# Remainders of weights on one engine, and scores of two attention jobs at once

## What is computed

```python
def first_block(x, ...):
    for i in range(2):
        h = rms_norm(x, norm_g[i])
        z = h @ w_in[i]
        z_a, z_b, z_c = split_cols(z, (RWKV_IN_WIDTH, DSA_IN_WIDTH, DIL_IN_WIDTH))
        y = jnp.concatenate([rwkv7_branch(z_a, ...), dsa_branch(z_b, ...), dilated_branch(z_c, ...)], axis=-1)
        x = x + y @ w_out[i]
        gate = jax.nn.sigmoid(rms_norm(x, ple_norm_g[i]) @ ple_w_gate[i])
        x = x + gate * (p[i] @ ple_w_proj[i])
    return rms_norm(x, final_norm_g)

def second_block(x, mem, ...):
    for l in range(2):
        h = rms_norm_2(x, attn_norm[l])
        # layer 0: o_mix = sparse attention (compressed, selected, windowed; 12 heads)
        # layer 1: o_mix = forgetting_attention(q, k_sh, v_sh, dcum)     (12 heads)
        o_mem = memory_attention(q_mem, mem, mem_norm[l], w_mem_kv[l])   # 4 heads
        x = x + jnp.concatenate([o_mix, o_mem], axis=-1) @ w_o[l]
        x = x + conv_ffn(rms_norm_2(x, ffn_norm[l]), w_up[l], conv_w[l], conv_b[l], w_down[l])
    return rms_norm_2(x, final_norm)

def conv_ffn(h, w_up, conv_w, conv_b, w_down):
    u = h @ w_up                                  # 1024 -> 2 x 2816
    u = causal depthwise convolution of width 3 over u, + conv_b
    a, b = u[..., :D_FF], u[..., D_FF:]
    return (jax.nn.silu(a) * b) @ w_down
```

## Time and profile before

| | |
|---|---|
| median of 3 runs | 1552.84 us (1551.9 to 1553.16) |
| the profiled execution, its own time | 1553.33 us |
| its span, first to last instruction | 1551.4 us |
| mean granted clock of TensorE | 0.853 of 2.4 GHz |
| HBM read, mean rate | 164.9 MB, 107 GB/s |

### The profile page before, as it was taken

How to read it: one execution, slowest core, us unless ns; L and a number is a source line. 1 busy time by engine, 2 the same in 40 slices (tenths; PEclk the granted TensorE clock), 3 DMA queues, 4 the chain that set the end, 5 groups by cost and what they waited for, 6 DMA issues and landing times.

```text
span 1551.4 us, 25100 instructions
## 1 busy us (share of the span) xinstructions
PE 1340.0 (86%) x10545; PEld 1223.1 (79%) x10545; DVE 897.6 (58%) x1579; ACT 648.6 (42%) x1144; POOL 495.3 (32%) x294
## 2 busy tenths in 40 slices
PE   3969885989698859879899899986988999999787
PEld 3957774988577749779777699885988878999787
DVE  1884647457746474557755446777436344588842
ACT  3533123465331235554532345454434333555541
POOL 1544100334440003346400224444545201344541
PEclk9989966999799659889855599998989856999989
DMA  6324100344330004326210144443534301444450
GB/s 242 133 102 141 56 2 1 114 159 136 109 131 29 2 1 169 130 82 234 73 55 1 44 147 136 136 154 131 182 132 139 132 1 55 139 161 163 153 179 35
DMA packets 24448, 167.56 MB, mean 108 GB/s; under 512 B 2704, under 2 KB 2832, under 8 KB 8336
## 3 DMA queue, kind: packets, MB, share of 16 engines
q1 hardware_dynamic: 24336, 165.96, 30.8%
HBM read 164.90 MB, written 1.05 MB: 107 GB/s over the span
## 4 chain that ended last, share of the span: by engine, by line
PE 37%; DVE 16%; ACT 7%; issue 2%; POOL 0%; DMA 0%; DVEq 0%; ACTq 0%; SPq 0%
PE ps L445 7%; PE ps L440 7%; PE ps L442 7%; DVE ARENA L2038 5%; PE ps L603 4%; PE ps L622 4%; DVE FR L399 3%; ACT FR L386 3%; DVE WL L399 2%; ACT WH L386 2%; PE ps L612 2%; DVE ARENA L2030 1%; PE ps L483 1%; PE ps L471 1%; PE ps L463 1%
## 5 line engine op out<-in xcount | busy, mean ns | idle before, releaser
L399 POOL TENSOR_TENSOR WL<-raw,WH 128x1024 fp32r<-128x1024 f32 (+3 forms) x105 | 246.6, 2349 | 385.4 <-ACT WH L386 385.3
L440 PE MATMUL ps<-FR,WH 128*128 128x256 f32 x1156 | 290.8, 290 | 43.4 <-ACT WH L386 28.8
L442 PE MATMUL ps<-FR,WH 128*128 128x256 f32 x1156 | 285.0, 285 | 2.3 <-DVE FR L504 1.3
L440 PEld LDWEIGHTS ps<-FR,WH 128*128 128x128 f32 x1156 | 222.5, 192 | 47.5 <-issue 31.9
L386 ACT ACTIVATE WH<-raw 128x1024 fp32r<-128x1024 f32 (+4 forms) x211 | 203.1, 984 | 132.6 <-PE ps L445 68.1
L399 DVE TENSOR_TENSOR WL<-raw,WH 128x1024 fp32r<-128x1024 f32 (+4 forms) x106 | 155.0, 1464 | 156.1 <-ACT WH L386 156.0
L440 PE MATMUL ps<-FR,FR 128*128 128x256 f32 x772 | 201.0, 296 | 30.1 <-ACT FR L508 22.9
L442 PEld LDWEIGHTS ps<-FR,WH 128*128 128x128 f32 x1156 | 222.5, 192 | 4.3 <-DVE FR L504 2.0
L442 PE MATMUL ps<-FR,FR 128*128 128x256 f32 x772 | 198.8, 292 | 4.3 <-DVE FR L512 3.7
L399 POOL TENSOR_TENSOR FR<-raw,FR 128x1024 fp32r<-128x1024 f32 (+2 forms) x58 | 141.4, 2441 | 137.7 <-ACT FR L386 137.7
L440 PEld LDWEIGHTS ps<-FR,FR 128*128 128x128 f32 x772 | 152.6, 198 | 35.5 <-ACT FR L508 21.5
(11 more groups left out here) (315 smaller groups left out, 2147.4 us busy)
## 6 DMA issues: line engine op xcount, KB each, us to landing
raw<-wst_in SPq DMA_DIRECT2D x123, 1024.0 KB, 4.9
raw<-wst_in SPq DMA_DIRECT2D x17, 896.0 KB, 4.6
raw<-wst_in SPq DMA_DIRECT2D x11, 768.0 KB, 4.3
raw<-wst_in SPq DMA_DIRECT2D x4, 912.0 KB, 4.6
cst<-cst_in SPq DMA_DIRECT2D x1, 1681.0 KB, 13.3
X<-xT_in SPq DMA_DIRECT2D x2, 512.0 KB, 4.4
ARENA<-memT_in SPq DMA_DIRECT2D x1, 1024.0 KB, 4.8
out_dram<-X SPq DMA_DIRECT2D x2, 512.0 KB, 2.6
```

Of the source, the lines that this page charges most:

```text
L399: e.tensor_tensor(lo[:, 0:cols], src, hi[:, 0:cols].bitcast(F32), SUB).then_inc(*put(LO[me], ("lo", i)))
L440: pe.matmul(out, hv[:, k, :], src.hi[:, c, :], start=k0 == 0 and k == ks[0], stop=False)
L442: pe.matmul(out, hv[:, k, :], src.lo[:, c, :], start=False, stop=False)
```

## The change

The remainders of all items are computed on VectorE: `lo_engine` goes, and so do GpSimd's calls of `split_lo` in seven functions. GpSimd keeps its other work. In each function of VectorE the call now covers even and odd items, at the same place and as far ahead.

In the attention each job with an even number has a mate, the job after it, on the other half of the partitions. Step 0 of the even job issues the scores of both, head by head in turn, into two banks of PSUM, and one semaphore increment marks both; step 0 of the mate issues nothing on TensorE. The order of sparse attention's jobs is changed so that neighbours lie on different halves. The steps are woven by pairs, three pairs at a time, and both jobs of a pair do the same step one after the other. The computed function stays the same.

```diff
@@ the semaphores
-    "split_hi": "A", "split_lo_v": "V", "split_lo_g": "G", "item_used": "PE",
+    "split_hi": "A", "split_lo": "V", "item_used": "PE",
...
@@ split_lo and its choice of engine
-    nxt = {"A": 0, "V": 0, "G": 0}
-    LO = {"V": "split_lo_v", "G": "split_lo_g"}
-
-    def lo_engine(i):
-        return "V" if i % 2 == 0 else "G"
+    nxt = {"A": 0, "V": 0}
...
-    def split_lo(e, q, me, *event, ahead=None):
-
-        while nxt[me] < items_until(event, ahead):
-            i = nxt[me]
-            nxt[me] += 1
+    def split_lo(v, q, *event, ahead=None):
+
+        while nxt["V"] < items_until(event, ahead):
+            i = nxt["V"]
+            nxt["V"] += 1
             cols, split = known.plan[i][1:]
-            if not split or lo_engine(i) != me:
+            if not split:
                 continue
             src, _ = raw_of(i)
             (hi, lo), _ = slot_of(i)
             q.wait_ge(*got("hi", i))
-            e.tensor_tensor(lo[:, 0:cols], src, hi[:, 0:cols].bitcast(F32), SUB).then_inc(*put(LO[me], ("lo", i)))
+            v.tensor_tensor(lo[:, 0:cols], src, hi[:, 0:cols].bitcast(F32), SUB).then_inc(*put("split_lo", ("lo", i)))
...
@@ attention jobs
     def placed(jobs, sms, pts):
+
         for n, j in enumerate(jobs):
             j.place(n, jobs, sms, pts)
+            j.mate = jobs[n + 1] if n % 2 == 0 else None
         return jobs
 
+    def by_pairs(units, width):
+
+        steps = weave([8 if u == ["compress"] else 4 for u in units], width)
+        return [(x, s) for n, s in steps for x in units[n]]
+
+    def two_each(jobs):
+        return [jobs[n:n + 2] for n in range(0, len(jobs), 2)]
+
     def attn_pe(j, s):
-        if s == 0:
-            for e in j.ready:
-                qpe.wait_ge(*got(*e))
+        if s == 0 and j.mate:
+            for x in (j, j.mate):
+                for e in x.ready:
+                    qpe.wait_ge(*got(*e))
             for h0, n in j.groups:
-                ps = begin_bank("S", j.id, h0)
+                pair = [begin_bank("S", x.id, h0) for x in (j, j.mate)]
                 for i in range(n):
-                    ins = pe.matmul(ps[:, j.nk * i:j.nk * i + j.nk], j.q(h0 + i), j.k(h0 + i), start=True, stop=True)
-                ins.then_inc(*put("attn_pe", ("S", j.id, h0)))
+                    for x, ps in zip((j, j.mate), pair):
+                        ins = pe.matmul(ps[:, j.nk * i:j.nk * i + j.nk], x.q(h0 + i), x.k(h0 + i), start=True, stop=True)
+                ins.then_inc(*put("attn_pe", ("S", j.id, h0), ("S", j.mate.id, h0)))
...
@@ layer_g, as in out_g, between_g, o_g, ffn_g, nsa_g and fox_g: GpSimd's calls go
             elif s[0] == "cols":
                 c0 = 2 * s[1]
-                split_lo(g_, q, "G", "cols", l, c0)
...
@@ NsaMap
-            slc, win = ([self.job(b, g, i0, kind) for b in (1, 0) for g in range(2) for i0 in (0, 2, 4)] for kind in (0, 1))
+            slc, win = ([self.job(b, g, i0, kind) for b in (1, 0) for i0 in (0, 2, 4) for g in range(2)] for kind in (0, 1))
...
-            self.all = ["compress"] + slc + win[:6] + [1, 0] + win[6:] + mem
-            steps = weave([8 if x == "compress" else 4 for x in self.all], 6)
-            self.steps = [(self.all[n], s) for n, s in steps]
+            self.steps = by_pairs([["compress"]] + two_each(slc + win[:6]) + [[1], [0]] + two_each(win[6:] + mem), 3)
...
@@ FoxMap
-            self.steps = [(self.jobs[n], s) for n, s in weave([4] * len(self.jobs), 6)]
+            self.steps = by_pairs(two_each(self.jobs), 3)
```

More of the change, by code:

```diff
@@ L1471, in layer_v @@
                 c0 = 2 * s[1]
-                split_lo(v, q, "V", "cols", l, c0)
+                split_lo(v, q, "cols", l, c0)
                 if c0 == 0:
@@ L1511, in layer_v @@
                 g, k = s[1:]
-                split_lo(v, q, "V", "rows", l, g, k)
+                split_lo(v, q, "rows", l, g, k)
                 if (g, k) == (0, 0):
@@ L1764, in out_v @@
         for c0 in range(0, 8, 2):
-            split_lo(v, q, "V", "w_out", l, c0)
+            split_lo(v, q, "w_out", l, c0)
             ps, free = psum("w_out", l, c0)
@@ L1773, in out_v @@
         for c0 in range(0, 8, 2):
-            split_lo(v, q, "V", "w_gate", l, c0)
-            split_lo(v, q, "V", "w_proj", l, c0)
+            split_lo(v, q, "w_gate", l, c0)
+            split_lo(v, q, "w_proj", l, c0)
             gate_pair_v(v, q, l, c0)
@@ L1843, in out_g @@
         barrier(q, "G", ("L", l))
-        for c0 in range(0, 8, 2):
-            split_lo(g_, q, "G", "w_out", l, c0)
-        for c0 in range(0, 8, 2):
-            split_lo(g_, q, "G", "w_gate", l, c0)
-            split_lo(g_, q, "G", "w_proj", l, c0)
         if l == 1:
@@ L1896, in between_v @@
                 .then_inc(*put("scaled", ("x fin", c), *([("mean free", ("in", 2))] if c == 7 else [])))
-        split_lo(v, q, "V", "mem k", 0)
-        split_lo(v, q, "V", "mem v", 0)
+        split_lo(v, q, "mem k", 0)
+        split_lo(v, q, "mem v", 0)
         B.mark("V", "end", "T", "V")
@@ L1952, in o_v @@
         barrier(q, "V", stage)
-        split_lo(v, q, "V", "w_o", l, 0, ahead=5)
+        split_lo(v, q, "w_o", l, 0, ahead=5)
         for c in range(8):
@@ L1957, in o_v @@
         for c0 in range(0, 8, 2):
-            split_lo(v, q, "V", "w_o", l, c0)
+            split_lo(v, q, "w_o", l, c0)
             ps, free = psum("w_o", l, c0)
@@ L1986, in o_g @@
     def o_g(g_, q, l):
-        for c0 in range(0, 8, 2):
-            split_lo(g_, q, "G", "w_o", l, c0)
         B.mark("G", "end", ("P", l), "G")
@@ L2023, in ffn_v @@
             if i < FC:
-                split_lo(v, q, "V", "up", l, i)
+                split_lo(v, q, "up", l, i)
                 if i == 0:
@@ L2100, in ffn_g @@
                 g_.tensor_tensor(m.fb[n % 3], u[0], u[1], MUL).then_inc(*put("ffn_g", ("f", l, n)))
-        for c0 in range(0, 8, 2):
-            split_lo(g_, q, "G", "down", l, c0)
         B.mark("G", "end", ("F", l), "G")
@@ L2296, in nsa_v @@
         for c0 in range(0, 6, 2):
-            split_lo(v, q, "V", "zc", c0)
+            split_lo(v, q, "zc", c0)
         for x in range(2):
@@ L2336, in compress_v @@
             if n < 2:
-                split_lo(v, q, "V", "cmp1", x, n)
+                split_lo(v, q, "cmp1", x, n)
             else:
@@ L2477, in nsa_g @@
         barrier(q, "G", "T")
-        split_lo(g_, q, "G", "mem k", 1)
         scaled_g(g_, q, m.H, "HN", m.hs)
-        split_lo(g_, q, "G", "mem v", 1)
-        split_lo(g_, q, "G", "nrows", 0)
-        split_lo(g_, q, "G", "nrows", 1)
-        for c0 in range(0, 6, 2):
-            split_lo(g_, q, "G", "zc", c0)
         fl = lambda x: x.rearrange("p v l n -> p (v l n)")
@@ L2487, in nsa_g @@
         g_.tensor_tensor(fl(m.Ul), fl(m.U), fl(m.Uh).bitcast(F32), SUB).then_inc(*put("cmp_g", ("Ul",)))
-        split_lo(g_, q, "G", "nrows", 2)
         for x, s in m.steps:
-            if x == "compress":
-                if s < 6 and s % 3 < 2:
-                    split_lo(g_, q, "G", "cmp1", s // 3, s % 3)
-            elif x not in (0, 1):
+            if x not in ("compress", 0, 1):
                 attn_g(g_, q, x, s)
@@ L2571, in fox_v @@
         for c0 in range(0, 6, 2):
-            split_lo(v, q, "V", "k pe", c0)
+            split_lo(v, q, "k pe", c0)
             ps, free = psum("k", c0)
@@ L2597, in fox_v @@
         for g in range(2):
-            split_lo(v, q, "V", "v pe", g)
+            split_lo(v, q, "v pe", g)
             ps, free = psum("v", g, 1)
@@ L2611, in fox_v @@
         for c0 in range(0, 8, 2):
-            split_lo(v, q, "V", "q pe", c0)
+            split_lo(v, q, "q pe", c0)
         for x, s in m.steps:
@@ L2651, in fox_g @@
         barrier(q, "G", ("F", 0))
-        split_lo(g_, q, "G", "forget")
         scaled_g(g_, q, m.HK, "HK", m.hs)
-        for c0 in range(0, 6, 2):
-            split_lo(g_, q, "G", "k pe", c0)
         scaled_g(g_, q, m.H, "HX", m.hs)
-        for g in range(2):
-            split_lo(g_, q, "G", "v pe", g)
-        for c0 in range(0, 8, 2):
-            split_lo(g_, q, "G", "q pe", c0)
         B.mark("G", "end", "X", "G")
```

19 lines of the change are left out of this document (6 added, 13 removed).

## The result

The changed kernel takes 1478.4 us (median of four runs, 1473.9 to 1481.2) against 1552.4: a ratio of 0.952, 95% interval 0.949 to 0.955. The prediction was 1498, so 20 us more went than forecast. The profiled execution took 1473.9 us with a span of 1472.0, the shortest of the four. Their spans go with the granted clock: 1472.0 at 0.879, 1474.7 at 0.874, 1478.3 at 0.870, 1479.2 at 0.869.

What follows compares the result with a forecast made beforehand. Bounds: ScalarE-VectorE rings in the up projections, TensorE near its lower clock in the second block's attention. 30 + 6 + 19 = 55 us off 1551.4 gave a span of 1496.4, so 1498 predicted; own range 1480 to 1510, wider 1460 to 1522.

Steps and rivals of the forecast that it cites:

- rival (a): In the attention the granted clock rises above 0.5, a further 18 to 37 us off: 1461 to 1480; chance 0.22.
- Ring of the up projections: Both feed-forward layers: the closed ScalarE-VectorE loop takes 6.12 us per iteration against 7.26 and 6.52, 30 us saved.
- Input projections: First block, both layers: VectorE's collisions with GpSimd's remainders go, about 3 us off per layer, 6 together.
- Everywhere else: Other projections: the 100 or so moved remainders cost nothing; bounds 4 us gained to 15 lost.
- rival (c): VectorE becomes late where TensorE is full (w_o, w_out, gates), 15 us lost there: 1510 to 1520; chance 0.08.
- The cover that I named: Outside the rings, 16 matmuls with the rounded part hide a moved remainder; without it, up to 1.15 us each.
- Overlap: Second block's attention: paired scores on two halves take 60% of serial time (bounds 50% and 70%), saving 28 us.
- Waits: Attention: the order by pairs adds 6 us behind score blocks and 3 us in the compressed branch, 9 together.
- The clock: Attention: the sum counted no gain from a higher granted clock, leaving that to rival (a).
- The attention term: Second block's attention: 28 us saved by paired scores less 9 us of waits, net 19 us; bounds 9 lost, 60 gained.

Runs made afterwards that it cites:

- up_alone: The kernel before with only the up projections' odd remainders moved from GpSimd to VectorE, all others still alternating: 1520.6 us (0.980).
- wide_only: The kernel before with each product with v of the second block streaming 128 columns of v instead of 64: 1521.9 us (0.980).
- same_half: The changed kernel with two of three attention pairs, and the memory pairs, having both jobs on the same half of the partitions: 1489.8 us (0.960).

## Why the prediction was right, and by how much not

The measured 1478.4 lies in the range that was stated, 1460 to 1522, but not in the forecast's own, 1480 to 1510: the range held because it took in rival (a). One step of the sum failed, the clock's; the others follow in the order of the sum.

- **Ring of the up projections, 6.12 us, 30 us saved.** Measured 6.10 and 31.7. Right in mechanism and size, and shown by `up_alone`: with these remainders alone the ring is there.
- **Input projections, 6 us.** Measured 2.8 + 4.5 = 7.3. The collisions went as said, but the place I named did not show it: TensorE's wait for the last L1500 fell only from 26.5 to 24.4 in two, not to 10 each. The gain came ahead of that wait and behind it.
- **Everywhere else, 0.** Measured +6.4 at the gates of the first block, -5.0 in its second recurrence (the clock's, in two profiled runs only, so no effect of the change that I can show), and at most 1 in any stage elsewhere. The mechanism of rival (c) is real, at one of the three places it named; w_o and w_out show nothing. The cover that I named, the 16 matmuls with the rounded part, hides the remainder from TensorE; it does not hide it from the evacuation behind it in VectorE's queue and from ScalarE, which splits again only after that.
- **Overlap, 60% of the serial time.** Measured 50% (2.08 against 2.07 for one job). The first block's 2.10 us for 12, which I read as 70% of the serial 3.0, was no measure of the halves: the same place takes 1.57 now. Full overlap was one of the bounds I had, and the block at half clock gives it. In us the term came out at 25.6 or 30, by the clock that it is priced at, against 28, because two errors cancel: the overlap was larger than I took it, and what it acts on was smaller. A pair of 256 keys saves 3.78 - 2.08 = 1.70 us and not 2.0, one of 128 keys 2.07 - 1.23 = 0.84 and not 1.0, and 13 x 1.70 + 9 x 0.84 = 29.7 at 1.2 GHz. (63% for my 60% would be worth 2 us of the 70 that are serial, not the 1 that I wrote.)
- **Waits, 9 us.** Measured 10.7 more idle time, at L620 on ScalarE's exponentials, as named, and at L630 on VectorE's copies, which I had not named.
- **The clock, 0. This is the step that failed.** The attention term was 19 = 28 - 9; it measured 40.3 = 25.6 + 25.4 - 10.7. The clock's 25.4 lies inside the 18 to 37 that rival (a) gave it, and 1478.4 is rival (a)'s time (1461 to 1480), not that of the forecast's own range (1480 to 1510). So the time was met by the rival, to which I gave 0.22, and not by the sum. I had set it low because the products with v stayed as sparse as before. They do, and `wide_only` shows that they hold the clock down; but they do not hold it at 1.2 GHz throughout once the rest of the stage changes. In the sparse attention the overlap of the scores brought most of the gain, in the forgetting attention it came with the order by pairs and stayed when most of the overlap was taken away (`same_half`), which neither my sum nor rival (a) had thought of. The trace before gave little warning: in the windows of the earlier trace rows TensorE had 2.4 GHz for 4 of 116 and 4 of 67 us. The 14 and 24 us of the table lie mostly ahead of them, 20 of the 24 in the last projections before 1232. A clock near its lower level is therefore a term of the sum, with bounds of its own, whenever a change reorders TensorE's work in that stage.

In sum: 31.7 + 7.3 + 40.3 + 5.0 + 1.5 - 6.4 = 79.4 us in the profiled run, 74.0 by the medians, where 55 were forecast.

## What to carry to other kernels

When a helper's work moves to an engine, look for every closed ring through that engine, not only for TensorE's waits: the move paid where it took a collision out of a ring (31.7 us) and cost where it put an instruction into one (6.4, of which putting it back gave 1.9 in one profiled run). Where TensorE is the bound at its lower clock, price three things apart: work, waiting and granted clock; the last can be nearly as large as what the edit was made for. Issue matmuls of 64 rows on both halves of the partitions next to one another; with up to four of one half in a row their order did not matter.

## What the runs showed of the hardware

- Two runs of score instructions on different halves of the partitions take the time of one: 2.08 us for eight and 2.07 for four at 1.2 GHz, even where the four of one half stand in the program ahead of the four of the other (2.09). With six ahead of six, at 2.4 GHz in the first block, the twelve took 2.10 us, and 1.57 with four at most in a row.
- More streamed columns made a stage shorter: 128 of v and not 64 added 5 us of work at 2.4 GHz and took 14.1 and 16.7 us off, by a granted clock of 0.73 for 0.55 and 0.93 for 0.63. Eight such products took 2.08 us for 1.97 at 1.2 GHz.
- VectorE does the remainders of both engines for 53 us more of its own busy time: a 128x1024 subtraction takes it 1.23 us, and up to 3.42 beside one of GpSimd's; four convolutions take 1.78 us alone and 3.35 beside it.
- The granted clock rose in the forgetting attention without most of the overlap: 0.77 over the stage with two pairs of three on one half, 0.78 with none, 0.63 before.
- The same program's time goes with the clock that it was granted: 1472.0 us of span at 0.879, 1479.2 at 0.869. In one place the same 24 products with v took 5.36 us in one kernel's profiled run and 3.04 in another's.
